# State-space decays: exponents of four heads as a rank-32 product plus a triangle product, one exponential for both directions

## The reference

```python
dt = softplus(dt + dt_bias)                       # 32 heads forward, 32 backward
a = (dt * a_neg)                                  # a_neg = -exp(a_log)
acum = cumsum(a, over the chunk)
lmat = exp(where(tri, acum[l] - acum[s], -inf))   # 128x128 for each head
cb = einsum('bclgn,bcsgn->bcgls', cc, bc)         # 128x128 for each group
y_diag = einsum('bcgrls,bcsgrp->bclgrp', cb * lmat, x * dt)
# + what crosses the chunk border, + the same on the flipped sequence, + x * d_skip
```

## Time and profile before

| | |
|---|---|
| time, median of 3 runs | 1426.09 us (1424.97 to 1430.47) |
| profiled execution, its own time | 1428.35 us |
| its span, first to last instruction | 1426.5 us |
| mean granted TensorE clock | 0.968 |
| PE busy in the span | 1349.1 us |
| DVE, ACT, POOL busy | 956.8, 725.4, 163.9 us |
| Mamba-2 stage | from about 934 to about 1227 us of the span |

### The profile page before, as it was taken

The page is one execution under the profiler, slowest core; times in us unless marked ns, Lnnn a source line. Parts: engine busy times, 40 slices in busy tenths (PEclk is TensorE's granted clock), DMA queues, the critical chain, the costliest instruction groups (busy, mean ns, idle before and its releaser), DMA issues.

```text
span 1426.5 us, 20118 instructions
## 1 busy us (share of the span) xinstructions
PE 1349.1 (95%) x8246; PEld 1187.5 (83%) x8246; DVE 956.8 (67%) x1122; ACT 725.4 (51%) x987; POOL 163.9 (11%) x195
## 2 busy tenths in 40 slices
PE   8999999998999999998899999989899888999997
PEld 7898888888888888788788888888888778888885
DVE  6766665567756655665866665697889885766565
ACT  4445544455555444434634444466767663344441
POOL 0000000005340000000000000011344352000000
PEclk9999999999799999999899999999999999999998
DMA  8564656634077666435045556634333313455552
GB/s 281 194 189 134 191 182 197 201 129 148 4 174 207 182 196 199 161 123 173 1 148 177 177 182 202 206 119 149 118 121 116 118 61 119 134 199 199 177 178 88
DMA packets 220315, 223.07 MB, mean 156 GB/s; under 512 B 7232, under 2 KB 204224, under 8 KB 220096
## 3 DMA queue, kind: packets, MB, share of 16 engines
q1 hardware_dynamic: 217472, 213.94, 46.6%
q10 hardware_dynamic: 1728, 5.76, 1.3%
q0 software_dynamic: 1024, 2.10, 0.9%
HBM read 220.72 MB, written 1.05 MB: 155 GB/s over the span
## 4 chain that ended last, share of the span: by engine, by line
PE 79%; DVE 13%; issue 3%; ACT 2%; POOL 2%; DMA 1%; POOLq 0%; DVEq 0%; SPq 0%; ACTq 0%
PE ps L415 23%; PE ps L515 19%; PE ps L417 12%; PE ps L427 4%; PE ps L428 4%; PE ps L429 4%; PE ps L770 3%; DVE ssm_taps L1570 3%; DVE wlo L1202 2%; DVE weight L1593 1%; PE ps L404 1%; PE ps L406 1%; PE ps L405 1%; PE ps L606 1%; PE ps L595 1%
## 5 line engine op out<-in xcount | busy, mean ns | idle before, releaser
L1202 DVE TENSOR_TENSOR wlo<-raw,whi 128x2048 fp32r<-128x2048 f32 x202 | 468.5, 2322 | 166.6 <-ACT whi L845 166.6
L415 PE MATMUL ps<-act,whi 128*128 128x512 f32 x1408 | 503.3, 401 | 8.8 <-DVE act L1240 4.9
L845 ACT ACTIVATE whi<-raw 128x2048 fp32r<-128x2048 f32 x202 | 385.2, 1908 | 70.0 <-PE ps L515 37.1
L417 PE MATMUL ps<-act,wlo 128*128 128x256 f32 x1408 | 397.4, 282 | 0.0
L415 PEld LDWEIGHTS ps<-act,whi 128*128 128x128 f32 x1408 | 266.8, 189 | 74.9 <-issue 7.2
L417 PEld LDWEIGHTS ps<-act,wlo 128*128 128x128 f32 x1408 | 268.6, 191 | 1.8
L897 ACT ACTIVATE low_sb<-ps 128x512 f32<-128x512 f32 x88 | 52.6, 598 | 240.1 <-PE ps L417 240.1
L1697 POOL TENSOR_SCALAR small<-small 128x2 f32<-128x2 f32 (+2 forms) x17 | 6.5, 382 | 1081.1 <-DVE small L1228 713.7
L1319 DVE TENSOR_TENSOR sum_sb<-ps,low_sb 128x512 f32<-128x512 f32 x88 | 60.6, 688 | 101.2 <-ACT low_sb L897 101.2
L515 PE MATMUL ps<-whi,hidhi 128*128 128x512 f32 x400 | 124.3, 392 | 0.0
L515 PE MATMUL ps<-wlo,hidhi 128*128 128x512 f32 x400 | 123.9, 391 | 0.0
(11 more groups left out here) (222 smaller groups left out, 2164.6 us busy)
## 6 DMA issues: line engine op xcount, KB each, us to landing
raw<-in_mlp_w SPq DMA_DIRECT2D x128, 512.0 KB, 4.4
raw<-in_ffn_w_gate_up SPq DMA_DIRECT2D x88, 512.0 KB, 5.0
raw<-in_ssm_w_in SPq DMA_DIRECT2D x50, 512.0 KB, 4.8
raw<-in_ffn_w_down SPq DMA_DIRECT2D x44, 512.0 KB, 4.9
raw<-in_conv_w_in SPq DMA_DIRECT2D x24, 512.0 KB, 5.9
raw<-in_attn_w_in SPq DMA_DIRECT2D x18, 512.0 KB, 4.7
raw<-in_ssm_w_out SPq DMA_DIRECT2D x16, 512.0 KB, 4.4
raw<-in_attn_w_qkv SPq DMA_DIRECT2D x12, 512.0 KB, 4.3
```

The costliest lines, as they stand in the source:

```text
L415: e.matmul(ps[:, b + f, :].rearrange("p (a n) -> p a n", a=2), hi[:, k, cols], act[:, :, k, :], start=k == 0, stop=False, skip_group_check ...
L417: last = e.matmul(ps[:, b + f, 0:T], lo[:, k, cols], act[:, 0, k, :], start=False, stop=k == KT - 1, skip_group_check=True)
L845: e.activation(whi[s][:, :], raw[s][:, :], ACT.Copy).then_inc(*rounded.up(c))
L1202: e.tensor_tensor(wlo[s][:, :], raw[s][:, :], f32(whi[s][:, :]), ALU.subtract).then_inc(*split.up(c))
```

## The change

The exponent is written as a matrix product. Once, at G = 0, the running sums S of a over each chunk (both directions, all heads) come from four more small float32 products of the triangle tables in `make_edge`. DVE `make_parts` forms ln(dt) - S and splits both that and S into a rounded part and a rest. PE `turn_parts` transposes these (four 128x128), DVE `make_rows` makes `exp_row` (rows that are either sums or ones), and ACT `make_cols` makes `exp_col` in eight Identity activations of 128x512 with a scale and a bias for each partition. An item's exponent, for one direction and four heads, is then a product over 32 partitions (`exp_row` by `exp_col`) plus a product of minus 2^100 times the identity with a triangle mask, which drives the other triangle to minus infinity. ln(dt) is inside the exponent, so dt need not be multiplied in. The two directions stand in banks 4 and 5; one exponential of 128x1024 takes both, DVE adds the halves and multiplies by the gram, which ACT now copies whole (`copy_gram`). The products of `decays` on PE are of the rounded type, not of float32. POOL no longer makes `cum`. Bank 5 is now used by items, so `turn_xs`, `turn_y` and `out_chunk` get other waits, and the first `turn_y` has three banks in place of four.

```diff
 PE
 def turn_xs(G):
-                            e.wait_ge(*xs_copied(G - 1, 1))
+                            e.wait_ge(*decayed(4 * G - 3))
 def make_edge():
+    for m in range(MT):
+        for d, mask in enumerate((le, ge)):
+            c = P + 64 * m + 32 * d
+            last = e.matmul(ps[:, TOP, c:c + 32], mask, part_of(a, m, d), start=True, stop=True)
+def turn_parts():
+    e.wait_ge(*parts_step("split"))
+    for n in range(4):
+        last = e.transpose(ps[:, 4, n * P:(n + 1) * P], ...exp_parts[:, n]..., ident)
 def decays(n):
-    e.wait_ge(*cum_made(n))
     if n:
         e.wait_ge(*decayed(n - 1))
-    for d, mask in enumerate((gt, lt)):
-        last = e.matmul(ps[:, 4, :], mask, cum[d][n % 2]..., start=d == 0, stop=d == 1)
+    else: (waits masks_made, rows_made, cols_made)
+    if n % 4 == 2 and n < 12:
+        e.wait_ge(*xs_copied(n // 4 + 1, 1))
+    p_ = slice(32 * (g // 2), 32 * (g // 2) + 32)
+    for d, mask in enumerate((mask_f, mask_b)):
+        out = ps[:, 4 + d, :].rearrange("p (u n) -> p u n", u=4)
+        e.matmul(out, minus[:, :], spread(mask[:, :], [0, 4], [1, P]), start=True, stop=False)
+        last = e.matmul(out, exp_row[p_, 2 * m + d, :], exp_col[g % 2][p_, 2 * m + d, :, :], start=False, stop=True)
 in step G = 0, k = 4, behind the chunk:
+                        if k == 4 and G == 0:
+                            turn_parts()
 ACT
 def make_dt():
+    e.activation(rate, rows[...], ACT.Exp)        # moved ahead of the first Ln
     e.activation(ln_, u_, ACT.Ln).then_inc(*dt_act.up("ln"))
-    e.activation(rate, rows[...], ACT.Exp).then_inc(*dt_act.up("rate"))
+    e.wait_ge(*dt_step("capped"))
+    e.activation(ln_dt, capped_dt, ACT.Ln).then_inc(*dt_act.up("ln_dt"))
+    for dst, src, scale in ((minus, ident, -2.0 ** 100), (mask_f, gt, 1.0), (mask_b, lt, 1.0)):
+        last = e.activation(dst[:, :], src, ACT.Copy, scale=scale)
+def make_cols():
+    e.wait_ge(*rows_made())
+    for u in range(8):
+        last = e.activation(exp_col[u // 4][:, :, u % 4, :], ps[:, 4, :]..., ACT.Identity,
+                            scale=column("sum_head", u), bias=column("less_head", u))
+def copy_gram(g):                              # first in steps k = 0 and k = 3
+    e.wait_ge(*gram(g))
+    if g >= 2: (waits crossed(2 * g - 3), made(2 * g - 3))
+    e.activation(gram_all[:, g % 2, :], ps[:, TOP, :], ACT.Copy).then_inc(*gram_copied.up(g))
 def decays(n):
-    for u in range(4):
-        last = e.activation(weight[:, par, u, :], gram_f[:, g % 2, m, :], ACT.Copy, scale=...dt...)
     e.wait_ge(*cum_summed(n))
-    e.activation(decay[:, par, :, :]..., ps[:, 4, :], ACT.Exp).then_inc(*decayed.up(n))
+    e.activation(decay[:, par, :, :], ps[:, 4:6, :], ACT.Exp).then_inc(*decayed.up(n))
 in step G = 0, k = 4, last:
+                        if k == 4 and G == 0:
+                            make_cols()
 DVE
 def make_dt():
+    e.tensor_scalar(capped_dt, dt, 1e-37, None, ALU.max).then_inc(*dt_step.up("capped"))
-def make_gram(g): (three 128x256 operations)
+def make_parts(): (five 128x128 operations, after make_edge in G = 0, k = 3)
+def make_rows(): (one 128x512 operation out of PSUM, after the taps in G = 0, k = 4)
 def decays(n):
-    (four scalar_tensor_tensor of 128x128, then the product with decay)
+    e.wait_ge(*decayed(n))
+    e.tensor_tensor(out, decay[:, par, 0, :], decay[:, par, 1, :], ALU.add).then_inc(*decays_added.up(n))
+    e.wait_ge(*gram_copied(g))
+    e.tensor_tensor(weight..., weight..., spread(gram_all[:, g % 2, m * (T + P):], [0, 4], [1, P]), ALU.mult)
 POOL
 def prepare(n):
-    for mask, d in ((le, 0), (ge, 1)):
-        last = e.tensor_tensor(cum[d][n % 2][:, :, :], spread(mask, ...), spread(head_cols(a, m, d, g), ...), ALU.mult)
 turn_y(0) on PE, ACT and DVE: OUT_BANKS[:3] for OUT_BANKS
 out_chunk: before chunk n == 3 of half 0, wait decayed(15)
```

More of the change, by code:

```diff
@@ L109, in build @@
         hidlo, _ = place("hidlo", [P, 3, 2, T], F32R)
-        table, _ = place("table", [P, TAB_N])
+        table, table_at = place("table", [P, TAB_N])
         params, _ = place("params", [P, PAR_N])
@@ L153, in build @@
         window, _ = place("ssm_window", [P, 2, 2, T + 4], offset=hid_at + 4096)
-        cum = [[place(f"cum_{d}{n}", [P, 4, P], offset=lnrow_at + 4096 * d + 2048 * n)[0] for n in range(2)]
-               for d in range(2)]
-        decay, _ = place("decay", [P, 2, 4, P], offset=h_at)
-        weight, _ = place("weight", [P, 2, 4, P], offset=h_at + 4096)
+        decay, _ = place("decay", [P, 2, 2, 4 * P], offset=h_at)
+        exp_parts, _ = place("exp_parts", [P, 4, 4, 4, 8], F32R, offset=hid_at + 8320)
+        minus, mask_f, mask_b = (place(f"mask{n}", [P, P], F32R, offset=hid_at + 8320 + 2048 + 512 * n)[0] for n in range(3))
+        weight, _ = place("weight", [P, 2, 4, P], offset=table_at + 4 * TAB["dist"])
+        exp_row, _ = place("exp_row", [P, 4, P], F32R, offset=table_at + 4 * TAB["dist"] + 4096)
+        exp_col = [place(f"exp_col{n}", [P, 4, 4, P], F32R, offset=(lnrow_at, shared + 27136)[n])[0] for n in range(2)]
         small_at = [64]
@@ L721, in decays @@
                 def decays(n):
-                    e.wait_ge(*cum_made(n))
+                    g, m = item(n)
                     if n:
                         e.wait_ge(*decayed(n - 1))
-                    for d, mask in enumerate((gt, lt)):
-                        last = e.matmul(ps[:, 4, :], mask, cum[d][n % 2][:, :, :].rearrange("p u n -> p (u n)"),
-                                        start=d == 0, stop=d == 1)
+                    else:
+                        e.wait_ge(*masks_made())
+                        e.wait_ge(*rows_made())
+                        e.wait_ge(*cols_made())
+                    if n % 4 == 2 and n < 12:
[5 more added lines that the diff above has]
+                        last = e.matmul(out, exp_row[p_, 2 * m + d, :], exp_col[g % 2][p_, 2 * m + d, :, :], start=False, stop=True)
                     last.then_inc(*cum_summed.up(n))
@@ L763, in out_chunk @@
                         e.wait_ge(*y_lo(half, KT - 1))
+                    elif n == 3 and half == 0:
+                        e.wait_ge(*decayed(15))
                     hi, lo = (w8(w[c % SLOTS]) for w in (whi, wlo))
@@ L800, in ssm @@
                     if k == 0:
-                        turn_y(0, OUT_BANKS)
+                        turn_y(0, OUT_BANKS[:3])
                         make_gram(7)
@@ L1629, in ssm @@
                             decays(n)
-                        if k in (0, 3) and G:
-                            make_gram(2 * G - 2 + k // 3)
                         lo(ssm_step(G, k) + 2)
@@ L1641, in ssm @@
                             make_edge()
-                make_gram(6)
+                            make_parts()
+                        if k == 4 and G == 0:
+                            make_rows()
                 for k in range(4):
@@ L1646, in ssm @@
                         turn_y(0)
-                        make_gram(7)
                     else:
@@ L1889, in shape_tables, with head_columns @@
     return out
+def head_columns():
+    part, head = np.arange(P) // 8 % 4, np.arange(P) % 8
+    of_head = head[:, None] == np.arange(8)[None, :]
+    is_sum, is_less = part[:, None] < 2, part[:, None] >= 2
+    return np.concatenate([of_head & is_sum, of_head & is_less, is_sum, is_less], 1).astype(np.float32)
 _WEIGHTS = ["x", "conv_w_in", "conv_w_out", "attn_w_qkv", "attn_w_o", "ffn_w_gate_up", "ffn_w_down", "attn_w_in_2",
```

121 lines of the change are left out of this document (63 added, 58 removed).

## The result

| | before | after |
|---|---|---|
| median of 6 runs, us | 1426.07 (1424.65 to 1430.47) | 1441.67 (1438.63 to 1445.52) |
| profiled execution, us | 1428.35 | 1444.34 |
| its span, us | 1426.5 | 1442.5 |
| granted PE clock, mean | 0.968 | 0.957 |

The changed kernel is slower: ratio 1.0106 [1.0083, 1.0129], +15.6 us. The forecast was 1428.3, no change; 1441.67 lies outside its range and is, almost to the microsecond, the figure of rival B.

A forecast was written before the change was run, and what follows sets the result against it. PE was taken to bound the kernel, busy 95% of the span. Set-up +13.7, loop -9.4 and tail -2.1 us sum to +2.2, taking the median from 1426.09 to 1428.3 us, no change; range 1417 to 1440.

The forecast's parts named there:

- rival B: In `decays`, each change to 32 partitions drains PE with nothing overlapped, 0.35 us a change: 1442 us, slower; chance 0.14.
- the price of a change of partitions: PE's decay products: 0.07 us a change, four changes an item, 0.28 us; bounds 0 and 0.35 a change.
- the low clock behind `turn_xs`: No term; at `turn_xs` only a new PE wait of 0.83 us, three times, 2.5 us, was forecast.
- the step on the decay products: PE's decays fall from 1.76 to 1.22 us, saving 0.54 an item, bounds 0.82 and -0.58.
- The set-up's waits: G = 0: PE waits longer before k = 3's chunk and the first gram; whole set-up +13.7 us, bounds 9 and 19.
- k = 3's chunk later: G = 0: ACT waits for DVE's dt and takes more work, so PE starts this chunk 2.4 us later.
- its end to the first gram: G = 0, from the k = 4 chunk: PE waits 8.9 us instead of 1.48; with the transposes +8.0 us.
- gram and chunk behind it: Work behind the first gram's stall runs at about half clock: +2.0 us.
- rival C: The set-up does not stop PE for long, +4 instead of +13.7 us: 1418.6 us; chance 0.12.
- The loop's waits: PE's waits for DVE's weights shrink: -4.1 us at k = 2, and -2.9 at k = 5, where the gram waits for SiLU.
- rival D: DVE's weights stay late through POOL's remaining work; three waits of 1.7 us stay: 1433 us; chance 0.10.
- The tail: Last four items: decays save 1.6 us, DVE's chain some 0.5; -2.1 us in all, bounds 0 and -4.

The follow-up runs named there:

- the one with two: Changed kernel with both triangle products first, then both 32-partition products, so two changes of partition count an item: median 1431.4 us, ratio to before 1.0031.
- the other repairs: Changed kernel with zeroed rows over 128 partitions, x in banks 6 and 7, second Ln and masks later, SiLU ahead of z; with later `make_cols`: 1400.72 us, ratio 0.9819.
- two of these repairs: Kernel before with x through banks 6 and 7 and the SiLU ahead of the next z: median 1420.2 us, ratio 0.9956.
- the wait alone: Kernel before with one added wait, three times: PE's decays of k = 4 wait for ACT's copy of x's second half; 1431.74 us, ratio 1.0013.
- full rows: Changed kernel, all decay products over 128 partitions: 1426.99 us, result not the reference's; made right with the other groups' rows zeroed: 1428.17 us.
- the later logarithm: Changed kernel with ACT's second Ln and three mask copies moved behind the taps of G = 0, k = 1: median 1430.81 us, ratio 1.0031.

## Why the prediction was wrong

Two terms of the sum failed: the price of a change of partitions (0.07 us taken, 0.19 to 0.20 measured, 6.5 us in all) and the low clock behind `turn_xs` (nothing taken, 9.1 us measured).

**The price of a change of partitions.** "I take 0.07, the value of the nearest row" stands in the step on the decay products. It is 0.19 to 0.20 us, measured from two sides, the one with no change and the one with two. That a change costs something was said, and the bounds held it (0 to 0.35); the term was mis-sized. The nearest row was not near: its 64-partition products are 256 wide, and the time of one was compared with the time of the next, not the starts with those of a group without a change. The cross-check that stood in the same paragraph, 0.63 - 0.47 = 0.16 us for a product's way through the array, was much closer. Rival B needed 0.17 to decide. The saving of 0.54 us an item became nothing: 9 x 0.54 = 4.9 us of the loop and 1.6 of the tail.

The Trainium skill, TensorEngine Tiling, section Key Properties, says that a change of the tiling mode drains the engine. The trace fits it, with 0.24 us of idle before the weight load behind each change and 0.19 to 0.20 us a change on PE's path. It does not show that a drain is the reason, since the same 0.24 us stand before loads around the float32 products of before, all over 128 partitions. The page gives no price, and the measurement stands.

**The clock behind `turn_xs` was missing.** The wait itself was priced at 0.83 us and cost 0.94. I gave a low clock to the long stalls of the set-up and none to 1.86 and 0.78 us with half a microsecond of work between them, although the trace of before had low clock in G = 3, behind waits of 1.74 and 1.86 us, and I did not ask what it came from. It adds 6.6 us in the loop, and 2.5 more in the k = 4 chunk of the set-up, which also lies behind `turn_xs`. There the wait of 1.47 us is needed (without it the chunk took 5.84 us) but does not do it alone, for it stands in the kernel before as well, with no low clock behind it; what else it needs was not found. This error is larger than the first. With the decays alone mis-sized the forecast would have been 1435, with this alone 1437, both inside the range; only together do they reach the measured time. So the figure of rival B was hit for another reason than B's: B had 13.4 us from changes at 0.35 us, where 6.5 came from them.

**The set-up's waits were right.** The stretch is +13.7 us; up to the gram 11.7 were predicted. The sum held nothing for 3.1 us of low clock (the k = 4 chunk, and 0.6 in the edge products), and waits 1.4 us shorter than predicted hid a part of it: by luck the total is nearer than its terms.

| step | predicted | measured |
|---|---|---|
| k = 3's chunk later | +2.4 | +1.9 |
| pace between this chunk and the edge products | +0.5 | +0.7 |
| edge products | +0.8 | +1.4 |
| k = 4 chunk at a low clock | 0 | +2.5 |
| its end to the first gram | +8.0 | +7.1 |
| gram and chunk behind it | +2.0 | +1.5 |

The columns' pace, 0.74 predicted, was 0.68. The later `make_cols` confirmed that ACT's order is the cause of the wait before the gram, and that this part of rival C was only a matter of where the call stands.

**The loop's waits were nearly right.** At k = 2, 5.5 us went instead of 4.1, and no wait for weights was left (rival D falls). From the k = 4 chunk to the gram 10.64 us were measured, 10.6 predicted.

**The tail** gave +0.6 instead of -2.1: 1.6 of the difference of 2.7 are the decays, and 0.9 is a term that the prediction put at nothing: with three banks in place of four, ten transposes and not eight stand behind PE's wait, with another wait of 0.23 us between them, 2.68 us instead of 1.76. The wait in `turn_y` stayed (4.84 us, 4.87): most of the 0.5 us of DVE's shorter chain did not reach PE. Why was not tried.

**The confidence.** The forecast's own range (1422 to 1434) rested on one row for a term that counts 48 times. With the change priced at 0.16, which was on the page, the decays would have saved 0.18 an item and rival B would have been nearly as likely as the forecast.

## What to carry to other kernels

Price a new kind of instruction by the distance between starts in a group like the one it will stand in, and when it counts dozens of times let the forecast go through the dearer of two cross-checks. Count the idle times that a short wait on TensorE puts close to each other, not only its length: the work behind them may run at half the clock. And when a rewrite frees the engine that bound, look at what it puts in the written order of the others: here 8 of 15 us came from where a call stood, and with that and the other repairs the rewrite ended 2% under the kernel before (the old decays with two of these repairs: 0.4%).

## What the hardware showed that was not expected

- A product over 32 partitions between products over 128 costs 0.19 to 0.20 us a change at full clock, in either direction: 1.68 us for four 512-wide products with four changes, 1.29 with two, 1.01 with none, and where there are changes 0.09 more in the chunk behind. The weight load behind a change starts after 0.24 us of idle time. Loads around float32 products of 128x512 do the same, with no change of partitions.
- Idle times of 1.86 and 0.78 us about half a microsecond apart lowered the granted clock from 1.00 to between 0.50 and 0.71, in windows of 4 or 5 us behind them, at 18 of 21 places, in the seven profiles that have both waits and nothing in them. G = 2 kept 1.00 with the wait alone, and G = 3 with full rows, twice. Fifteen products of zeros in the two waits kept it at 1.00, and gave back 10.0 us.
- One execution of a kernel is not enough to price such a stretch: the kernel with the later logarithm gained 3.3 us between the grams, where it had no edit.
